# The last group's second up matrix as one transfer and one multiply: a two-layer mixture-of-experts encoder on one core

## The reference

```python
def expert_block(args):
    xi, e = args
    return (jax.nn.silu(xi @ w1[e]) * (xi @ w3[e])) @ w2[e]
# w1, w3: 1024 x 512 for each of 32 experts; w2: 512 x 1024
for i in range(DEPTH):                       # 2 layers
    h = rms_norm(x, norm_mix[i])
    ...
    x = x + jnp.concatenate([mix, att], axis=-1) @ w_out[i]
    x = x + hierarchical_moe(rms_norm(x, norm_ffn[i]), ...)
return rms_norm(x, final_norm)
```

## Time and profile before

| | us |
|---|---|
| median of 3 runs | 1133.85 |
| the three runs | 1133.08 to 1134.19 |
| the profiled execution | 1133.13 |
| its span | 1131.3 |
| TensorE busy | 867.1 (77%) |
| VectorE, ScalarE busy | 168.7 (15%), 177.3 (16%) |
| moved by DMA | 444.51 MB, 393 GB/s on average |

### The profile page before, as it was taken

How to read it: one execution, slowest core, us unless ns; L and a number is a source line. 1 busy time by engine, 2 the same in 40 slices (tenths; PEclk the granted TensorE clock), 3 DMA queues, 4 the chain that set the end, 5 groups by cost and what they waited for, 6 DMA issues and landing times.

```text
span 1131.3 us, 11631 instructions
## 1 busy us (share of the span) xinstructions
PE 867.1 (77%) x5176; PEld 407.6 (36%) x5176; DVE 168.7 (15%) x340; ACT 177.3 (16%) x399; POOL 19.2 (2%) x20
## 2 busy tenths in 40 slices
PE   9999998747668765575899999984758567465766
PEld 7688443312323221121258665431222222121222
DVE  2222241000010000000015543200000000000001
ACT  3323221000010100000035441100010101010102
POOL 0600000000000000000000000000000000000000
PEclk9999999888888888788899999997889879797979
DMA  9972799999999999999995668999999999999997
GB/s 372 420 316 86 288 417 425 429 428 446 434 427 432 443 419 439 439 420 423 424 422 210 265 243 335 415 429 447 432 431 432 436 432 431 436 423 440 434 410 289
DMA packets 24186, 444.51 MB, mean 393 GB/s; under 512 B 3137, under 2 KB 3649, under 8 KB 6594
## 3 DMA queue, kind: packets, MB, share of 16 engines
q1 hardware_dynamic: 23552, 443.17, 92.6%
q10 hardware_dynamic: 578, 0.52, 0.1%
HBM read 442.63 MB, written 1.05 MB: 392 GB/s over the span
## 4 chain that ended last, share of the span: by engine, by line
DMA 52%; PE 44%; ACT 1%; DVE 1%; issue 1%; SPq 0%; DVEq 0%
DMA ring<-in_joined 40%; PE ps L1162 13%; PE ps L1166 6%; DMA ring<-in_moe_w 6%; DMA ring<-in_last_down 5%; PE ps L908 4%; PE ps L1372 4%; PE ps L987 3%; PE ps L1465 2%; PE ps L994 2%; PE ps L1431 1%; DMA xres<-in_x 1%; PE ps L1104 1%; PE ps L1438 1%; PE ps L1340 1%
## 5 line engine op out<-in xcount | busy, mean ns | idle before, releaser
L1162 PE MATMUL ps<-ring,work 128*32 128x512 f32 x2008 | 271.8, 700 | 191.9 <-DMA ring<-in_joined 167.7
L1162 PEld LDWEIGHTS ps<-ring,work 128*32 128x32 f32 x2008 | 75.4, 126 | 379.9 <-issue 287.5
L1166 PE MATMUL ps<-ring,work 128*32 128x512 f32 (+1 forms) x1024 | 128.4, 656 | 30.8 <-DMA ring<-in_joined 20.0
L1166 PEld LDWEIGHTS ps<-ring,work 128*32 128x32 f32 x1024 | 38.2, 121 | 110.1 <-issue 80.4
L2217 DVE SCALAR_TENSOR_TENSOR work<-ps,st,work 128x512 f32<-128x512 f32 x16 | 12.0, 749 | 397.3 <-ACT work L1764 397.3
L1104 PE MATMUL ps<-xres,work 128*128 128x512 f32 x112 | 51.8, 605 | 9.5 <-ACT work L1768 9.5
L908 PE MATMUL ps<-ring 128*128 128x384 f32 x160 | 53.3, 489 | 0.0
L1764 ACT ACTIVATE work<-ps,st 128x512 f32<-128x512 f32 x16 | 11.0, 687 | 242.1 <-PE ps L1162 242.1
L2220 DVE SCALAR_TENSOR_TENSOR work<-ps,st,work 128x512 f32<-128x512 f32 x16 | 12.0, 750 | 228.3 <-PE ps L1162 228.3
L1766 ACT COPY work<-ps 128x256 f32<-128x256 f32 x16 | 6.0, 372 | 246.6 <-PE ps L1203 246.6
L1372 PE MATMUL ps<-ring 128*128 128x256 f32 x192 | 43.0, 382 | 0.0
(11 more groups left out here) (284 smaller groups left out, 712.6 us busy)
## 6 DMA issues: line engine op xcount, KB each, us to landing
ring<-in_moe_w SPq DMA_DIRECT2D x40, 2048.0 KB, 14.9
ring<-in_last_up SPq DMA_DIRECT2D x8, 2048.0 KB, 33.8
ring<-in_moe_w SPq DMA_DIRECT2D x15, 1024.0 KB, 7.3
ring<-in_out SPq DMA_DIRECT2D x4, 2048.0 KB, 27.6
ring<-in_first_up SPq DMA_DIRECT2D x4, 2048.0 KB, 12.0
ring<-in_last_down SPq DMA_DIRECT2D x4, 2048.0 KB, 37.5
ring<-in_queries_keys SPq DMA_DIRECT2D x7, 1024.0 KB, 25.5
ring<-in_first_up SPq DMA_DIRECT2D x4, 1024.0 KB, 7.3
```

The costliest lines, as they stand in the source:

```text
L1162: return pe.matmul(ps[32 * e:32 * e + 32, up_bank + m, :], xsel[:, k, 32 * e:32 * e + 32], w, start=k == 0, stop=k == KC - 1, tile_positio ...
L1166: return pe.matmul(ps[32 * e:32 * e + 32, bank, 0:w.shape[-1]], actT[:, j, 32 * e:32 * e + 32], w, start=j == 0, stop=j == 3, tile_positio ...
```

## The change

Matrix 22 of either layer becomes a joined matrix: `joined` gets one more matrix per layer, `last_up` goes away, and the last group's second up matrix takes the path of a whole matrix in `quad`, as in the other groups. It takes the side that is its turn: slots 2 to 5 in layer 0, 6 to 9 in layer 1. The down slices, which keep their form, go to other slots: 0, 1, 8, 7 in place of 4, 5, 8, 7 in layer 0, and 0, 1, 10, 3 in place of 7, 8, 9, 3 in layer 1.

```diff
-LAST_HOMES = ((0, 1, 2, 3, 4, 5, 8, 7), (0, 1, 10, 6, 7, 8, 9, 3))
+LAST_HOMES = ((0, 1, 8, 7), (0, 1, 10, 3))
 FIRST_JOINED = (2 * 3 + 2, 2 * 3)
-SLICED = [(0,)] + [()] * (NQ - 2) + [(1, 2)]
+SLICED = [(0,)] + [()] * (NQ - 2) + [(2,)]
...
-    up = o["moe_w3"][:, NE - E4:NE].reshape(2, E4, P, 4, 2 * FF)
-    o["last_up"] = np.stack([up[:, :, :, f].transpose(0, 2, 1, 3).reshape(2, P, SLOT) for f in range(4)], axis=1)
...
-                                      for i in range(FIRST_JOINED[1], 3 * (NQ - 1) + 1)]) for l in range(2)])
+                                      for i in range(FIRST_JOINED[1], 3 * NQ - 1)]) for l in range(2)])
...
         def joined_at(l, g, w):
-            return FIRST_JOINED[l] <= 3 * g + w <= 3 * (NQ - 1)
+            return FIRST_JOINED[l] <= 3 * g + w < 3 * NQ - 1
...
-                        slots += LAST_HOMES[l][(w - 1) * E4:w * E4]
+                        slots += LAST_HOMES[l]
...
-                    sp.dma_start(slot_view(slot), (first_up, last_up, last_down)[w][l, i]).then_inc(rn.ring_in[slot], 16)
+                    sp.dma_start(slot_view(slot), (last_down if w else first_up)[l, i]).then_inc(rn.ring_in[slot], 16)
```

More of the change, by code:

```diff
@@ L199, in build @@
           values0, queries_keys0, values1, values1_second, mem_queries1, queries_keys1, gates1, out0, out1, gains,
-          logit_weights, logit_biases, gate_biases, gate_ups, biases0, first_up, last_up, last_down, joined, out):
+          logit_weights, logit_biases, gate_biases, gate_ups, biases0, first_up, last_down, joined, out):
     with ExitStack() as ctx:
@@ L2449 @@
          "out0", "out1", "gains", "logit_weights", "logit_biases", "gate_biases", "gate_ups", "biases0", "first_up",
-         "last_up", "last_down", "joined"]
+         "last_down", "joined"]
```

## The result

| | before | changed |
|---|---|---|
| median, us | 1133.65 (6 runs) | 1144.1 (6 runs) |
| lowest to highest | 1132.5 to 1134.5 | 1142.56 to 1144.79 |
| ratio | | 1.0089 (1.0079 to 1.0100) |
| profiled execution, its span | 1133.13, 1131.3 | 1144.26, 1142.5 |

The account below looks back on a forecast made before the run. The prediction took expert-weight DMAs to bound both layers, with TensorE bounding layer 1's mixer between. Later ends of 5.47 us (layer 1) and 5.38 (layer 0), homes 0, sum to 10.9 on the 1133.85 median: 1144.7 us, range 1139.3 to 1148.3.

Parts of the forecast that it names:

- the likeliest case: Both layers' last groups end later because the second up multiply waits for the whole matrix: 1144.7 us, given 70%.
- Transfers: Second up matrix of each last group: whole, it lands 19.46 us behind matrix 21, 0.2 us later than the fourth slice.
- The "nothing" for the form of the transfer: Last group's second up matrix: one DMA in place of four saves three issues per layer, worth nothing.
- Second up multiply: Last group of each layer: its 64 records start only when all has landed and take 9.4 us, bounds 7.07 and 9.93.
- The step to the down part: From the end of the second up multiply until the transposed activations are in SBUF: 2.44 us.
- The down part at TensorE's own pace: Last group: waits for down transfers vanish; 10.27 us to layer 0's scatter, 13.18 to layer 1's last piece.
- The homes: New slots of layer 0's down slices, which layer 1's mixer loads wait for: cost 0, bound +0.5 us.
- Sum: Later ends of both layers: 5.47 us in layer 1 plus 5.38 in layer 0, 10.9 in all.
- Full pass through the mixer: Layer 1's mixer: TensorE passes on layer 0's delay of 5.38 us, and layer 1's expert loads follow.
- The rival by which nothing of layer 0's delay would be left: Layer 1's experts, paced by the DMA stream, absorb layer 0's delay; only layer 1's 5.5 us stays: 1139.3, 9%.
- The rival of the quicker stream: Between matrices 21 and 22: long runs land 8 MB so early that the multiply is hidden; 1130 at 12 us per matrix, 2%.

Follow-up runs that it names:

- experiment 1: Kernel before, its four 2 MB transfers and slots kept, but TensorE waits for all four slices before the second up matrix's first matmul: 1144.13 us, ratio 1.0084.
- experiment 8: Kernel before with all 30 joined matrices brought in four 2 MB transfers each, same wait and slots: 1140.0 us against 1133.33, ratio 1.0058.
- experiment 4: Changed kernel with six matmuls on constants before TensorE's wait for matrix 22 in the last group of either layer: 1139.36 us, ratio 1.0053.
- experiment 2: Kernel before, still sliced, but with the slots of the change: 1133.48 us, ratio 0.9988.
- experiment 3: Kernel before with the change in one layer: layer 0 alone 1138.41 us, layer 1 alone 1138.23; repeated beside the full change (1144.44): 1138.1 and 1138.49.

## Why the prediction was right

The forecast was 1144.7 us; measured are 1144.1, and it was the likeliest case that came true, by its mechanism too: the multiply behind the landing is the cost (experiment 1). By its own steps:

- **Transfers.** I had the whole matrix landing 19.46 us behind matrix 21, and it took 19.25 in both layers, as long as the four slices (19.27 and 19.26). 19.46 was an average with some long steps in it. The "nothing" for the form of the transfer holds here: experiment 8 gives 0.22 us per matrix in favour of the long runs, 0.4 us for the two of this change, less than experiment 1 (1144.13) can tell from the change (1144.1).
- **Second up multiply.** 9.4 us forecast; 9.53 and 8.87 measured. Experiment 1 shows that it is the cause, experiment 4 that its length over 7.07 us is the clock's.
- **The step to the down part.** 2.44 us forecast; 567.01 - 555.05 - 9.53 = 2.43 and 1120.63 - 1109.32 - 8.87 = 2.44.
- **The down part at TensorE's own pace.** 10.27 us to the scatter in layer 0 forecast, 577.28 - 567.01 = 10.27 measured. Its waits went, as said. One reading in it was wrong: the prediction puts the 1.7 us that layer 0 gets back down to the clock of its first down slice. Experiment 2 had that slice at 1.93 us and its scatter came only 0.2 us earlier, for the down transfers set the pace in the kernel before. What either layer got back is slack behind the landing, as in layer 1, where the down part starts 7.06 us later by the forecast and costs 5.47. The sum is the same.
- **The homes.** SP issued mem_queries1 at 569.00 (569.1 forecast), the mixer did not wait, and experiment 2 shows no cost (its interval reaches 1 us).
- **Sum.** Layer 0 5.38 forecast, 5.17 measured at the scatter (577.28 against 572.11); layer 1 5.47 forecast, 4.70 measured from matrix 21 to the end, by the shorter landing and multiply.
- **Full pass through the mixer.** 130.98 us in both kernels, and with the change in layer 0 alone the time rose by 4.6 and 4.1 us. The rival by which nothing of layer 0's delay would be left is refuted by that; that a part of it is absorbed is not excluded (experiment 3). In the profiled execution 1.3 us came on top in the experts, which I had not forecast; it made up for the shorter end of layer 1, and since that stretch was 372.77 in another profile of the same kernel, that this execution (1144.26) is so near to the 1144.0 of the sum is in part luck. By the means of the profiles the two ends cost 10.1, by the medians 10.45, against 10.9 forecast.

The rival of the quicker stream failed. The Trainium skill's fit for a single DMA on the GpSimd path ("DMA: Bandwidth & Descriptors", section on the anatomy of one DMA) has some 2 us for each transfer besides its bytes; for transfers queued behind each other from SP, experiment 8 measured 0.074 us, so the fit does not carry over to this stream. In direction the table of its section Bandwidth, 341 GB/s at 1 MB and 425 at 16 MB, agrees with the 428 and 434 GB/s here: longer transfers are quicker.

## What to carry to other kernels

In a kernel like this one, the last matrix before a chain of dependent work should land in pieces that are multiplied as they come, even where joined transfers are the better form for the rest (experiment 8): earlier groups hide the multiply under the next transfer, the last one has only the slack of what follows. To size the pieces, add up TensorE's work from the landing to the end and hold it against the transfers still on their way; up to there a coarser piece is free (two halves stand just beyond it, at 0.8 us by the medians and 1.8 by the profile), beyond it every microsecond counts, and filling matmuls that stood in waits begin to count as well. A multiply that starts after an idle time has to be priced by rows of the same situation: in all 14 profiles, a whole matrix multiplied after a wait of 5.2 us or more took 8.3 us or longer, against 7.07 at the full clock.

## What the runs showed of the hardware

- 90 more transfers in the queue cost 6.7 us, 0.074 us each, their shorter runs included: 8 MB with 64 KB runs moved at 434 GB/s, in four transfers with 16 KB runs at 428. Joined matrix or 2 MB slice, a transfer was cut into 144 packets, 128 with one run each and 16 short ones.
- The length of the wait alone does not tell the clock behind it. In the kernel before, these two down matrices follow the same work; the granted clock in their first 2 us was 0.50 after a wait of 1.20 us and 1.00 after one of 2.44:

```profile
830.02 8.71 PE L1166 MATMUL ps<-ring,work 128*32 128x512 f32 x64 [1.20 <-DMA ring<-in_joined]
1064.10 7.07 PE L1166 MATMUL ps<-ring,work 128*32 128x512 f32 x64 [2.44 <-DMA ring<-in_joined]
```

- The stream has long steps of its own. In most cases one joined matrix follows the last by 19.24 to 19.46 us (24 of 28 steps in the changed kernel's profile, 14 of 27 in that of the kernel before); but every profile has one to three steps of 20.2 to 20.9. In the timeline of the changed kernel one lies between these two:

```profile
952.95 8.55 PE L1164 MATMUL ps<-ring,work 128*32 128x512 f32 x64 [1.36 <-DMA ring<-in_joined]
973.84 8.35 PE L1160 MATMUL ps<-ring,work 128*32 128x512 f32 x64 [8.70 <-DMA ring<-in_joined]
```

  It took 20.89 us. What causes them was not tried. They are of the size by which executions of one kernel differ (1142.56 to 1144.79 for the changed kernel), so a difference of one or two us between two single profiles tells nothing.
